# First stage of a decoder step: weight piece 0 in two halves, sums of squares moved off TensorE's start

## The reference, cut to what matters

```python
def rmsnorm(x, g):
    xf = x.astype(jnp.float32)
    y = xf * lax.rsqrt(jnp.mean(xf * xf, axis=-1, keepdims=True) + RMS_EPS)
    return (y * g.astype(jnp.float32)).astype(x.dtype)

def a_qkv(x, pos, norm_g, w_qkv, qn, kn):
    n, t, _ = x.shape
    qkv = (rmsnorm(x, norm_g) @ w_qkv).reshape(n, t, 3, N_HEADS_A, HEAD_DIM)
    q = rope(rmsnorm(qkv[:, :, 0], qn), pos)
    k = rope(rmsnorm(qkv[:, :, 1], kn), pos)
    return q, k, qkv[:, :, 2]
```

## Time and profile before

| what | us |
|---|---|
| median of 3 runs | 1412.44 |
| lowest and highest run | 1411.72, 1413.26 |
| profiled execution, its own time | 1412.59 |
| its span, first to last instruction | 1410.9 |
| TensorE busy in it | 1389.5 |
| VectorE, ScalarE, GpSimd busy | 456.2, 325.8, 173.3 |

### The profile page before, as it was taken

One profiled execution on the slowest core, in us unless ns is written; L12 is line 12 of the kernel. 1 busy time (PEld: TensorE's weight loads), 2 busy tenths in 40 slices (PEclk: granted clock), 3 DMA queues, 4 the chain that ended last, 5 costly groups with the idle time before them and its releaser, 6 DMA issues.

```text
span 1410.9 us, 35332 instructions
## 1 busy us (share of the span) xinstructions
PE 1389.5 (98%) x16009; PEld 841.7 (60%) x16009; DVE 456.2 (32%) x964; ACT 325.8 (23%) x629; POOL 173.3 (12%) x218
## 2 busy tenths in 40 slices
PE   9999999999999899999999999999999999999997
PEld 7885999999998573353353353353354354344344
DVE  7967666664587541120120120120120120120111
ACT  6446544344453642001001001001001001001000
POOL 5623320000165611000000000000000000000100
PEclk9999999999999999999999999999999999999999
DMA  8959795535755378999999999999999999999993
GB/s 268 317 171 318 253 360 181 158 109 164 252 179 190 112 301 352 408 418 418 410 418 420 407 418 419 410 418 420 407 418 419 408 419 420 409 419 419 401 420 144
DMA packets 146427, 471.62 MB, mean 334 GB/s; under 512 B 9760, under 2 KB 81824, under 8 KB 117472
## 3 DMA queue, kind: packets, MB, share of 16 engines
q1 hardware_dynamic: 138544, 439.48, 79.6%
q0 software_dynamic: 7728, 29.82, 5.8%
HBM read 451.17 MB, written 18.09 MB: 333 GB/s over the span
## 4 chain that ended last, share of the span: by engine, by line
PE 95%; DVE 2%; ACT 1%; issue 1%; DMA 1%; SPq 0%; DVEq 0%; ACTq 0%
PE psum L1220 41%; PE psum L1260 21%; PE psum L367 9%; PE psum L368 9%; PE psum L369 9%; PE psum L929 1%; PE psum L993 1%; PE psum L865 1%; PE psum L914 1%; PE psum L954 1%; DMA raw<-in_w_qkv_a 1%; PE psum L972 1%; DVE p_b L1697 0%; PE psum L856 0%; PE psum L1204 0%
## 5 line engine op out<-in xcount | busy, mean ns | idle before, releaser
L1220 PE MATMUL psum<-wexp,xg 128*32 128x512 f32 (+1 forms) x6144 | 579.2, 539 | 0.0
L1220 PEld LDWEIGHTS psum<-wexp,xg 128*32 128x32 f32 x6144 | 199.4, 110 | 374.8 <-issue 373.3
L1260 PE MATMUL psum<-wexp,act 128*32 128x256 f32 x5376 | 291.5, 379 | 0.0
L2063 DVE TENSOR_TENSOR am<-sg,psum 128x512 f32<-128x512 f32 (+1 forms) x48 | 26.9, 616 | 731.7 <-issue 485.2
L1260 PEld LDWEIGHTS psum<-wexp,act 128*32 128x32 f32 x5376 | 174.8, 110 | 117.0 <-issue 3.1
L367 PE MATMUL psum<-hh,whi 128*128 128x288 f32 x696 | 207.4, 298 | 0.0
L368 PE MATMUL psum<-hl,whi 128*128 128x288 f32 x696 | 205.4, 295 | 0.0
L369 PE MATMUL psum<-hh,wlo 128*128 128x288 f32 x696 | 205.1, 295 | 0.0
L363 DVE TENSOR_TENSOR wlo<-raw,whi 128x2048 fp32r<-128x2048 f32 (+1 forms) x66 | 144.6, 2192 | 54.4 <-ACT whi L359 54.3
L367 PEld LDWEIGHTS psum<-hh,whi 128*128 128x128 f32 x696 | 130.9, 188 | 8.5 <-issue 8.3
L368 PEld LDWEIGHTS psum<-hl,whi 128*128 128x128 f32 x696 | 130.9, 188 | 0.1
(11 more groups left out here) (304 smaller groups left out, 1052.3 us busy)
## 6 DMA issues: line engine op xcount, KB each, us to landing
wexp<-in_w_moe SPq DMA_DIRECT2D x224, 1024.0 KB, 11.6
wexp<-in_w_moe SPq DMA_DIRECT2D x128, 768.0 KB, 10.8
raw<-in_w_gu_dense SPq DMA_DIRECT2D x22, 1024.0 KB, 5.6
wexp<-in_w_moe SPq DMA_DIRECT2D x32, 512.0 KB, 12.6
raw<-in_w_qkv_a SPq DMA_DIRECT2D x12, 1024.0 KB, 12.8
raw<-in_w_down_dense SPq DMA_DIRECT2D x16, 704.0 KB, 4.5
raw<-in_w_q_b SPq DMA_DIRECT2D x6, 1024.0 KB, 5.0
h_rows<-zeros POOLq DMA_DIRECT2D x14, 384.0 KB, 10.1
```

The costliest lines, as they stand in the source:

```text
L1220: ins = nc.tensor.matmul(ps[NG * part + r][32 * j:32 * j + 32, 0:wd], xg[:, r, 32 * k:32 * k + 32], wexp[:, q % RING, wd * j:wd * j + wd], ...
L1260: ins = nc.tensor.matmul(ps[6 + r // 2][32 * j:32 * j + 32, 256 * (r % 2):256 * (r % 2) + 256], act[:, r, 32 * kk:32 * kk + 32], wexp[:, q ...
L2063: V.tensor_tensor(am[:, r, 0:wd], sg[:, r, 0:wd], ps[NG + r][:, 0:wd], ALU.mult).then_inc(sem("gated_up"), 1)
```

## The change

- SyncE no longer issues the gains; ScalarE issues them itself, at its start.
- Piece 0 comes in two transfers of four rows k each (`first_half`, then the ring's own counter). Each half has its own high split on ScalarE (`first_high`, then `hi_ready`) and its own low split on VectorE (`first_low`, then `pieces_split`). The first tile takes its products in the same order, with a wait at k = 0 and k = 4 in each of its two runs.
- featsum is issued behind piece 1.
- GpSimd squares x tiles 0 to 3 into `hn`, ScalarE tiles 4 to 7 into `late_sq` after its high splits of piece 0 and ahead of that of piece 1. GpSimd adds all eight into `hn[:, 0]`, each add after the one ahead of it (`x_added`).
- The eight products featsum x square at TensorE's start go. One product, `first_total`, stands behind the second tile; it waits for featsum and the seventh add. `norm_root` moves into ScalarE's `project`, behind its work on tile 1.
- Seven warm matmuls instead of four; TensorE's wait for featsum ahead of them goes.
- The counters added_wo, added_dn and added_wob become one (`added`), k_stored and v_stored of both layers one each. GpSimd waits for its adds before the value load at r = 8.

```diff
@@ -135,6 +135,7 @@
         sq = at("sq", 49152, [P, KD, T])
+        late_sq = at("late_sq", 80000, [P, KD // 2, T])
         hn = at("hn", 58368, [P, KD, T])
...
@@ -383,7 +384,7 @@
         G0, F0 = CONST["g_attn_a"][0], CONST["featsum"][0]
-        POOL_SQ, WARM = 6, 4
+        POOL_SQ, WARM = 4, 7
         ROW_SQ, ROW_ADD = 3 * KD - POOL_SQ, 2 * (KD - 1)
...
@@ -391,6 +392,10 @@
             return KD * NORMS[tag] + k + 1
+
+        def added(tag, n):
+
+            return KD * ("wo", "dn", "wob").index(tag) + n
...
@@ -486,12 +491,12 @@
         def _(eng):
-            eng.dma_start(cst[:, G0:NCONST], io["const"][:, G0:NCONST]).then_inc(sem("gains_loaded"), 16)
             eng.dma_start(xT[:, 0:KD // 2, :], io["xT"][:, 0:KD // 2, :]).then_inc(sem("x_loaded"), 16)
             eng.dma_start(xT[:, KD // 2:KD, :], io["xT"][:, KD // 2:KD, :]).then_inc(sem("x_rest"), 16)
+            for half, landed in enumerate((sem("first_half"), raw_loaded[0])):
+                eng.dma_start(raw_view(0, KD, 2 * P)[:, 4 * half:4 * half + 4], W[0][:, 4 * half:4 * half + 4]).then_inc(landed, 16)
+            load_piece(eng, 1, W[1])
             eng.dma_start(cst[:, F0:F0 + P], io["const"][:, F0:F0 + P]).then_inc(sem("sum_loaded"), 16)
-            for p in range(2):
-                load_piece(eng, p, W[p])
             for lo, hi in ((0, F0), (F0 + P, G0)):
...
@@ -596,9 +601,14 @@
             for k in range(POOL_SQ):
-                if k == KD // 2:
-                    eng.wait_ge(sem("x_rest"), 16)
-                nc.gpsimd.tensor_tensor(sq[:, k], xT[:, k], xT[:, k], ALU.mult).then_inc(sem("x_squared"), 1)
+                nc.gpsimd.tensor_tensor(hn[:, k], xT[:, k], xT[:, k], ALU.mult).then_inc(sem("x_squared"), 1)
+            for k in range(1, KD):
+                eng.wait_ge(sem("x_squared"), min(k + 1, POOL_SQ))
+                if k > 1:
+                    eng.wait_ge(sem("x_added"), k - 1)
+                if k >= POOL_SQ:
+                    eng.wait_ge(sem("norm_squared"), k - POOL_SQ + 1)
+                nc.gpsimd.tensor_tensor(hn[:, 0], hn[:, 0], hn[:, k] if k < POOL_SQ else late_sq[:, k - POOL_SQ], ALU.add).then_inc(sem("x_added"), 1)
             eng.wait_ge(sem("pages_loaded"), 16)
...
@@ -618,7 +628,7 @@
                     eng.dma_start(out[P * lo:P * hi, :].rearrange("(j p) t -> p j t", p=P), b["kT"][:, lo:hi, :])\
-                        .then_inc(sem(f"k_stored_{b['tag']}"), 16)
+                        .then_inc(sem("k_stored"), 16)
...
@@ -659,6 +669,8 @@
                 pages.append(page_number(eng, r))
+                if r == 8:
+                    eng.wait_ge(sem("x_added"), KD - 1)
                 if 8 <= r < 12:
...
@@ -692,7 +704,7 @@
             norm_add("norm_b", KD - 1)
-            eng.wait_ge(sem("added_dn"), KD)
+            eng.wait_ge(sem("added"), added("dn", KD))
             eng.wait_ge(sem("out_stored"), 16)
...
@@ -771,9 +783,8 @@
                                                  bass.IndirectOffsetOnAxis(ap=rowi[0:w, 2 + i, c:c + 1], axis=0)).then_inc(sem("rows_moved"), 16)
-            for b in "ab":
-                eng.wait_ge(sem(f"k_stored_{b}"), 32)
-                eng.wait_ge(sem(f"v_stored_{b}"), 32)
+            eng.wait_ge(sem("k_stored"), 64)
+            eng.wait_ge(sem("v_stored"), 64)
...
@@ -781,20 +792,15 @@
                 nc.tensor.matmul(ps[1 if i else 6][:, :], warm[:, 0:P], warm[:, :], start=True, stop=True)
-            eng.wait_ge(sem("sum_loaded"), 16)
             def take(p):
                 eng.wait_ge(pieces_split, p + 1)
-            def norm_sum(tag, k):
-
-                if k < POOL_SQ:
-                    eng.wait_ge(sem("x_squared"), k + 1)
-                else:
-                    eng.wait_ge(sem("norm_squared"), k - POOL_SQ + 1)
-                ins = nc.tensor.matmul(ps[7][:, 0:T], con("featsum"), sq[:, k], start=k == 0, stop=k == KD - 1)
-                if k == KD - 1:
-                    ins.then_inc(sem("norm_summed"), 1)
+            def first_total():
+
+                eng.wait_ge(sem("sum_loaded"), 16)
+                eng.wait_ge(sem("x_added"), KD - 1)
+                nc.tensor.matmul(ps[7][:, 0:T], con("featsum"), hn[:, 0], start=True, stop=True).then_inc(sem("norm_summed"), 1)
...
@@ -803,13 +809,17 @@
-                eng.wait_ge(hi_ready, 1)
+                eng.wait_ge(sem("first_high"), 1)
                 for k in range(KD):
+                    if k == KD // 2:
+                        eng.wait_ge(hi_ready, 1)
                     eng.wait_ge(sem("norm_lo_ready"), norm_count("norm_a", k))
                     nc.tensor.matmul(ps[0][:, 0:T], whi[:, 0, 2 * k * P:2 * k * P + P], hh[:, k], start=k == 0, stop=False)
                     nc.tensor.matmul(ps[0][:, 0:T], whi[:, 0, 2 * k * P:2 * k * P + P], hl[:, k], start=False, stop=False)
-                take(0)
+                eng.wait_ge(sem("first_low"), 1)
                 for k in range(KD):
+                    if k == KD // 2:
+                        take(0)
                     ins = nc.tensor.matmul(ps[0][:, 0:T], wlo[:, 0, 2 * k * P:2 * k * P + P], hh[:, k], start=False, stop=k == KD - 1)
...
@@ -844,8 +854,11 @@
                         ins.then_inc(tile_sem(tiles, m), 1)
-                        if m == 1 and b is B:
-                            norm_total("norm_b", 2 * KD - 2)
+                        if m == 1:
+                            if b is A:
+                                first_total()
+                            else:
+                                norm_total("norm_b", 2 * KD - 2)
                     if m % 4 == 0 and 1 <= m // 4 <= nrot // 4:
...
@@ -1068,8 +1081,6 @@
-            for k in range(KD):
-                norm_sum("norm_a", k)
             project(A, tiles_a, lambda m: ("norm_a", hh, hl))
...
@@ -1286,7 +1297,6 @@
         def _(eng):
-            eng.wait_ge(sem("gains_loaded"), 16)
             done = [0]
...
@@ -1325,6 +1335,8 @@
                             .then_inc(sem(f"gained_{tg}"), 1)
+                        if m == 1 and b is A:
+                            norm_root("norm_a")
                     if m % 4 == 1 and 1 <= m // 4 <= 4:
...
@@ -1466,6 +1478,8 @@
+            eng.dma_start(cst[:, G0:NCONST], io["const"][:, G0:NCONST]).then_inc(sem("gains_loaded"), 16)
+            eng.wait_ge(sem("gains_loaded"), 16)
             nc.scalar.activation(rt[:, 0, 0:1], eps, ACT.Sqrt)
...
@@ -1473,10 +1487,15 @@
                 norm_hi("g_attn_a", k, hh)
+            half = KD * P
+            eng.wait_ge(sem("first_half"), 16)
+            nc.scalar.activation(whi[:, 0, 0:half], raw[:, 0, 0:half], ACT.Copy).then_inc(sem("first_high"), 1)
+            eng.wait_ge(raw_loaded[0], 16)
+            nc.scalar.activation(whi[:, 0, half:PIECE], raw[:, 0, half:PIECE], ACT.Copy).then_inc(hi_ready, 1)
+            done[0] = 1
             for k in range(POOL_SQ, KD):
-                square(k)
+                nc.scalar.activation(late_sq[:, k - POOL_SQ], xT[:, k], ACT.Square).then_inc(sem("norm_squared"), 1)
             split_upto(1)
-            norm_root("norm_a")
             project(A, tiles_a, lambda r: qs[:, 0:1] if r < 8 else gain("kn_a", 0))
...
@@ -1771,7 +1790,7 @@
-                        eng.wait_ge(sem(f"k_stored_{tg}"), 32)
+                        eng.wait_ge(sem("k_stored"), 32 if b is A else 64)
                     V.tensor_tensor(b["olo"][:, j, 0:SEQ], pv_out(b, j), b["ohi"][:, j, 0:SEQ].bitcast(F32), ALU.subtract)\
...
@@ -1851,6 +1870,12 @@
                 norm_lo("norm_a", "g_attn_a", k, hh, hl)
+            half = KD * P
+            eng.wait_ge(sem("first_high"), 1)
+            V.tensor_tensor(wlo[:, 0, 0:half], raw[:, 0, 0:half], whi[:, 0, 0:half].bitcast(F32), ALU.subtract).then_inc(sem("first_low"), 1)
+            eng.wait_ge(hi_ready, 1)
+            V.tensor_tensor(wlo[:, 0, half:PIECE], raw[:, 0, half:PIECE], whi[:, 0, half:PIECE].bitcast(F32), ALU.subtract).then_inc(pieces_split, 1)
+            done[0] = 1
             split_upto(1)
```

More of the change, by code:

```diff
@@ L633, in store_values @@
                 eng.wait_ge(sem(f"vtok_done_{b['tag']}"), b["nj"])
-                eng.dma_start(out[0:SEQ, :].rearrange("(b p) n -> p b n", p=P), b["vtok"][:, 0:2, :]).then_inc(sem(f"v_stored_{b['tag']}"), 16)
-                eng.dma_start(out[SEQ:T, :], b["vtok"][0:NSAMP, 2, :]).then_inc(sem(f"v_stored_{b['tag']}"), 16)
+                eng.dma_start(out[0:SEQ, :].rearrange("(b p) n -> p b n", p=P), b["vtok"][:, 0:2, :]).then_inc(sem("v_stored"), 16)
+                eng.dma_start(out[SEQ:T, :], b["vtok"][0:NSAMP, 2, :]).then_inc(sem("v_stored"), 16)
             def value_load(b, n):
@@ L835, in project @@
                         elif b is B:
-                            eng.wait_ge(sem("added_dn"), m + 5)
+                            eng.wait_ge(sem("added"), added("dn", m + 5))
                         name, xh, xl = sources(m)
@@ L1038, in router @@
                     eng.wait_ge(sem("router_scaled"), 1)
```

(20 more changed lines are left out.)

## The result

| | before | after |
|---|---|---|
| median of 20 runs each, us | 1413.03 | 1417.53 |
| lowest and highest, us | 1411.0, 1417.15 | 1412.17, 1421.1 |
| profiled execution, own time, us | 1412.59 | 1419.34 |
| its span, us | 1410.9 | 1417.6 |
| mean granted TensorE clock in it | 0.998 | 0.994 |

The ratio is 1.0029, with a 95% interval from 1.0019 to 1.0038: the changed kernel is slower by about 4 us, outside the predicted range.

The account below looks back on a forecast made before the run. TensorE, busy 98% of the span, was taken as the bound. Seventh add at 18.35 us plus product 0.48 and a semaphore step put the third tile at 18.9 instead of 19.23: 1412.44 - 0.3 = 1412.1 us, range 1410.5 to 1413.3.

Parts of the forecast that it names:

- Low splits: VectorE, piece 0: eight hl end at 11.4 us, half low splits 1.2 us each, first tile done at 14.4 to 14.8.
- rival 3, the clock: TensorE gaps between 9.8 and 14.9 us drop the second tile's clock, costing about 1.6 us: 1413.7 us; chance 0.05.
- The granted clock under 1 between 10 and 20 us: Sign listed as showing the forecast wrong: TensorE's granted clock below full in that stretch of the start.
- Gains by ScalarE's queue: Front of SyncE's queue: x and all behind it 0.46 us earlier, bounds 0 to 0.46, if data moves up with issue.
- Squares and adds: ScalarE's squares, then GpSimd's adds: seventh add done at 18.35 us, bounds 15.0 to 19.1, ahead of the single product.
- Rival 1: GpSimd's adds finish behind piece 1's low split: third tile at 19.3 to 19.6 us, 0.1 to 0.4 slower, 1412.7; chance 0.18.
- the single product: TensorE, between the second and third tile: the one product replacing the eight at the start costs 0.48 us there.
- The constants as next bound of the second tile: End of the first tile: constants land at 14.85 us, so the second tile starts at 14.9, capping the halves' gain.
- The high halves: ScalarE's two half splits of piece 0, ready at 9.55 and 11.05 us instead of 12.52 for the whole.
- the finish line: Start of TensorE's third tile, 19.23 us before the change; behind it the order of TensorE's work is unchanged.
- a span that moves by more than the third tile does: Sign listed as showing the forecast wrong: the whole span changes by more than the third tile's start.

Follow-up runs that it names:

- Two versions whose first stage is over 1 us ahead at the third tile: Wait for the constants moved to their first reader: in the kernel before with halves alone, 1413.22 us; in the changed kernel with adds and product later, 1413.33 us.
- the 93 runs above: 20 runs of the changed kernel and 73 of before, span against granted clock on one slope: changed kernel 2.2 us above at an equal clock.

## Why the prediction was wrong, point by point

**Wrong: "Low splits".** This is the step that failed. I let the `hl` end at 11.4 us and gave the halves 1.2 us each, 14.2 for the second "with a turn of GpSimd between them". They ended at 13.09, and the halves took 1.82 each. I had both prices in hand (0.50 alone, 0.92 beside GpSimd) and put them together by assuming gaps in the adds. The trace has one, of 0.62 us, which let a single `hl` through at 0.51; beside the adds the others took 1.04 to 1.07 us, more than my dear rate. From start to start that is 0.88 us each; eight of these are 7.04 us, past even my bound of 12.8 at the end because the first started at 6.05 and not at 5.5. The half splits I priced with at most one turn of GpSimd in all; each of them paid one. The size of a turn is one number throughout: 1.03 - 0.51 for an `hl`, 1.82 - 1.21 for a half, 2.88 - 2.29 for piece 1's split, so 0.5 to 0.6 us per instruction of VectorE. By halving the split the change doubled the number of turns. I looked at who blocks GpSimd, since the adds stood last in my sum, and not at whom GpSimd blocks.

By the Trainium skill, SBUF — State Buffer, section "SBUF: two separate sides", the shared pair of ports is locked by whoever starts first and for a whole instruction. The trace agrees: the price is one turn of the other engine for each instruction (0.5 to 0.6 us), whether VectorE's own takes 0.51 or 2.29 us, and it is gone where GpSimd is quiet (1.21 us a half with the adds later).

**Wrong: rival 3, the clock, in its chance.** Its price was right (1.6 us named, 1.32 measured at the second tile), its chance of 0.05 was not. I set a gap of 0.8 us before a tile at the full rate against it. With the `hl` and halves late there were three gaps, of 0.5, 1.2 and 1.0 us, within 4 us. It hung on the failed step and should have been carried along with its late end. The run with the gaps filled shows it as the cause of the second tile's 4.49 us. The granted clock under 1 between 10 and 20 us, which I had listed as a sign against me, came true.

**Wrong: "Gains by ScalarE's queue".** I took 0.46 us and named 0 as the other bound; x landed 0.15 us later than before in this pair (5.38 against 5.23), and over all the traces 0.04 us earlier on average. The condition that I had put on it, that the queue's data moves up as the issue does, failed for x and held for the weights (0.43 us at the second tile with the gains alone).

**Wrong: "Squares and adds".** I took the seventh add at 18.35 us and thought the third tile would wait for it. It was done at 17.24, within my bounds, and by then the tile was later than the adds. Rival 1 did not occur: the loss has the right sign and the other mechanism.

**Right:** the single product on the path at 0.48 us. The constants as next bound of the second tile: hidden in the changed kernel, where the tile is later, and shown with 0.8 us where the adds come later. First tile at 9.8 us (10.01). The high halves, ready at 9.96 and 11.48 us (9.55 and 11.05 forecast), were not the bound. And the finish line: 3.23 us lost at the third tile were still 3.2 us at the dense layer's down projection. One reading was short: a second group of waits belongs to the start, 1.6 us for `warm` ahead of the warm matmuls; it is the same in both kernels.

**Also wrong: the third tile as the only thing to move.** The sign listed against me, "a span that moves by more than the third tile does", came true, by 6.7 against 3.2 us in the profiled pair. A kernel slower by over 2.8 us, which I had given 0.03, is what was measured. The second attention falls to the lower clock for longer or shorter in eight of the eleven executions profiled here (mean 0.66 to 1.00 in 490 to 500 us). Whether a start that is 3 us later makes those falls longer is not shown: filling the gaps at the start brought the mean clock back from 0.9951 to 0.9975, more than the 0.0013 that the second tile's fall accounts for (0.09 x 20 us of the stretch 10 to 30 us, of 1418), but the runs scatter by 0.002 or more each. That part, about 1 us, stays open.

## What to carry to other kernels

Work moved to GpSimd is paid by VectorE, up to a whole turn at a time, where VectorE's instructions take two tiles from SBUF, as the `hl` and the splits do: count these instructions in the stretch, not their microseconds, and a split into two halves counts twice. Instructions with one such input did not pay: VectorE's 32 shuffles in the projection took 0.47 to 0.50 us each, with GpSimd busy beside them or not.

```profile
L1672 DVE STREAM_SHUFFLE sq<-hn x32: 469/480/495, 22.5 to 447.4; 128x288 f32<-128x288 f32 x32
```

Put the adds behind the stretch that sets the end (here: one wait and a later product, and the whole loss was gone), or leave them on an engine with slack. And carry a late end of one step on into the clock: a chain that makes TensorE wait in two places near each other can cost the tile behind them half its rate for a time (here 1.32 us).

## What the runs showed that I had not expected

A kernel's time at a fixed code differs by up to 9 us between runs, and most of it is the granted clock: 1410.5 us of span at 1.000, 1419.3 at 0.992. Two versions whose first stage is over 1 us ahead at the third tile showed no gain in the median of 12 runs, against such a scatter. Spans compared at an equal granted clock tell a change of 1 to 2 us apart better than medians do: the line through the 93 runs above gave 2.2 us to within 0.4, where the spans of after alone scatter by 9.

The move of a 22.5 KB load to another engine's queue about doubled its time (1.8 to 1.9 us in four traces, 3.3 to 3.9 in seven), and the 576 KB transfers beside it took 4.6 to 5.2 instead of 4.4 to 4.5 us. By the Trainium skill, DMA: Bandwidth & Descriptors, section "Issuing engines are not separate DMA queues", transfers of all issuing engines interleave on the same DMA engines, and a second issuer saves its issue time alone. The traces agree as far as x goes: 0.46 us of issue saved, none of it left at x's landing on average.
